# Convolution stage: the branch's early products as three fp32r products each, moved behind the fourth forward transform, and a ring of three PSUM banks

## The reference, cut to what matters

```python
y_a = _hyena(zx[..., :OFF_Q], ...)         # for o, gate in (x1, x2): y = gate * (irfft(rfft(y) * kf[o]) + bias * y)
y_b = _window_attention(q, k, v, kc, vc, attn_sink)
x_new = x + g1 * ((ga * (y_a @ w_branch_a) + gb * (y_b @ w_branch_b)) @ w_out)
x_new = x_new + g2 * _expert_choice(...)   # 16 experts, top-k of the tokens each
```

## Time and profile before

| what | us |
|---|---|
| median of 3 runs (2128.19 to 2129.42) | 2128.59 |
| the profiled execution's own time | 2128.68 |
| its span in the trace | 2126.8 |
| PE busy in the span | 2088.9 |
| convolution stage, 677.3 to 828.4: its length | 151.1 |

### The profile page before, as it was taken

The page is one execution under the profiler, slowest core; times in us unless marked ns, Lnnn a source line. Parts: engine busy times, 40 slices in busy tenths (PEclk is TensorE's granted clock), DMA queues, the critical chain, the costliest instruction groups (busy, mean ns, idle before and its releaser), DMA issues.

```text
span 2126.8 us, 28086 instructions
## 1 busy us (share of the span) xinstructions
PE 2088.9 (98%) x10361; PEld 1689.1 (79%) x10361; DVE 1667.5 (78%) x1784; ACT 1205.9 (57%) x1321; POOL 243.3 (11%) x106
## 2 busy tenths in 40 slices
PE   8999999989999999999999999999999999999998
PEld 6988888866679785787688888888888888888886
DVE  4577765158885987855898988889988989889986
ACT  4521222156622332334487787777877777877875
POOL 2000000000000012200620222102220122102200
PEclk9999999999999999999899999999999999999999
DMA  9144454130012457443899999999999999999993
GB/s 330 35 128 167 137 187 152 50 130 16 16 50 109 139 139 252 149 177 100 329 400 409 401 401 401 389 399 384 374 379 397 392 377 377 382 404 380 381 375 110
DMA packets 191371, 547.98 MB, mean 258 GB/s; under 512 B 17069, under 2 KB 67599, under 8 KB 190656
## 3 DMA queue, kind: packets, MB, share of 16 engines
q1 hardware_dynamic: 179512, 508.92, 63.5%
q0 software_dynamic: 6992, 23.29, 4.7%
q10 hardware_dynamic: 4792, 14.74, 1.9%
HBM read 504.97 MB, written 35.66 MB: 254 GB/s over the span
## 4 chain that ended last, share of the span: by engine, by line
PE 72%; DVE 3%; DMA 2%; ACT 1%; issue 1%; POOL 0%; POOLq 0%; SPq 0%; ACTq 0%; DVEq 0%
PE p_y L347 6%; PE p_y L349 5%; PE p_y L348 5%; PE p_b L347 5%; PE p_b L349 5%; PE p_b L348 5%; PE p_a L347 5%; PE p_a L349 5%; PE p_a L348 5%; PE p_j L1634 2%; PE p_m L347 2%; PE p_m L349 2%; PE p_m L348 2%; PE p_acc L2019 2%; PE p_o L1519 2%; PE p_t L3177 1%
## 5 line engine op out<-in xcount | busy, mean ns | idle before, releaser
L3044 DVE TENSOR_TENSOR r_lo<-ring,r_hi 128x2048 fp32r<-128x2048 f32 x372 | 838.8, 2287 | 57.5 <-ACT r_hi L2992 56.3
L2992 ACT ACTIVATE r_hi<-ring 128x2048 fp32r<-128x2048 f32 x372 | 708.5, 1916 | 149.3 <-PE p_b L349 72.9
L347 PE MATMUL p_y<-r_hi,a_hi 128*128 128x512 f32 x512 | 205.3, 401 | 0.0
L349 PE MATMUL p_y<-r_hi,a_lo 128*128 128x512 f32 x512 | 200.0, 391 | 0.0
L348 PE MATMUL p_y<-r_lo,a_hi 128*128 128x512 f32 x512 | 199.2, 389 | 0.0
L347 PE MATMUL p_a<-r_hi,x_hi 128*128 128x512 f32 x500 | 198.6, 397 | 0.0
L347 PE MATMUL p_b<-r_hi,x_hi 128*128 128x512 f32 x504 | 196.7, 390 | 0.1
L348 PE MATMUL p_b<-r_lo,x_hi 128*128 128x512 f32 x504 | 196.1, 389 | 0.0
L349 PE MATMUL p_b<-r_hi,x_lo 128*128 128x512 f32 x504 | 196.1, 389 | 0.0
L349 PE MATMUL p_a<-r_hi,x_lo 128*128 128x512 f32 x500 | 195.1, 390 | 0.0
L348 PE MATMUL p_a<-r_lo,x_hi 128*128 128x512 f32 x500 | 194.6, 389 | 0.0
(11 more groups left out here) (441 smaller groups left out, 3868.9 us busy)
## 6 DMA issues: line engine op xcount, KB each, us to landing
ring<-in_w_gate SPq DMA_DIRECT2D x128, 1024.0 KB, 10.7
ring<-in_w_up SPq DMA_DIRECT2D x128, 1024.0 KB, 10.0
ring<-in_w_down SPq DMA_DIRECT2D x128, 1024.0 KB, 12.6
ada_rest<-in_ada_w SPq DMA_DIRECT2D x16, 1024.0 KB, 5.4
w_raw<-in_w_in SPq DMA_DIRECT2D x15, 1024.0 KB, 7.4
h_parts<-in_ada_w SPq DMA_DIRECT2D x16, 512.0 KB, 9.1
gate_dram<-zs ACTq DMA_DIRECT2D x16, 512.0 KB, 2.6
x_normed<-gate_dram SPq DMA_DIRECT2D x16, 512.0 KB, 4.3
```

What stands on the lines that cost most here:

```text
L347: pe.matmul(out, a_hi, b_hi, start=start, stop=False)
L349: return pe.matmul(out, a_lo, b_hi, start=False, stop=stop)
L2992: act.activation(r_hi[:, i % PARTS], ring[:, i % RAW], ACT.Copy).then_inc(hi_ready, 1)
L3044: dve.tensor_tensor(r_lo[:, i % PARTS], ring[:, i % RAW], r_hi[:, i % PARTS].bitcast(F32), ALU.subtract).then_inc(lo_ready, 1)
```

## The change

`branch(j)` uses `three` on `w2_hi`/`w2_lo` and on the split `y2`: twelve fp32r matmuls of 512 columns in place of four fp32 ones, into one bank of `p_branch`. ACT makes the high parts (`rows_high` once, `columns_high(j)` eight times, into a single buffer `w2_hi`, so that it waits for the branch before), DVE the low parts (`rows_low` once, `columns_low(j)` eight times), and `branch(j)` waits for its low part. The freed bank goes to `pj`, a ring of three. The branches move: none ahead of forward 2; 0 after forward 3; two after each pair; 6 and 7 after back 6. SP's queue puts the loads of the merge's operands and of the gates in another order.

```diff
-        pj = ps("p_j", [P, 2, 512])
-        p_b = ps("p_branch", [P, 2, 512])
+        pj = ps("p_j", [P, BANKS, 512])
+        p_b = ps("p_branch", [P, 512])
...
             load_gate(0)
             load_columns(2)
+            load_gate(1)
             load_columns(3)
             load_columns(4)
-            load_gate(1)
-            load_columns(5)
             load_merge_input(0, g["yb"][:, :, 512:L], g["yb_dram"][:, 512:L])
             load_gate(2)
+            load_columns(5)
+            load_merge_input(1, g["wa"][:], A["w_branch_a"][0])
             load_columns(6)
-            load_merge_input(1, g["wa"][:], A["w_branch_a"][0])
+            load_merge_input(2, g["wb"][:], A["w_branch_b"][0])
             load_gate(3)
             load_columns(7)
-            load_merge_input(2, g["wb"][:], A["w_branch_b"][0])
...
-                        pe.wait_ge(emptied, n - 1)
+                        pe.wait_ge(emptied, n - BANKS + 1)
...
             def branch(j):
-                if j == 0:
-                    pe.wait_ge(y2_in, 16)
-                pe.wait_ge(w2_in[j % 2], 16 * (j // 2 + 1))
-                if j >= 2:
-                    pe.wait_ge(branch_read, j - 1)
+                pe.wait_ge(early_low, j + 3)
+                if j:
+                    pe.wait_ge(branch_read, j)
                 for c in range(NCH):
-                    mm = pe.matmul(p_b[:, j % 2], w2[:, j % 2, c, :], y2[:, c, :], start=c == 0, stop=c == NCH - 1)
+                    high = y2_halves[c // 2][1]
+                    mm = three(pe, p_b[:], w2_hi[:, c, :], w2_lo[:, j % 2, c, :], high[:, c % 2], y2_lo[:, c, :],
+                               c == 0, c == NCH - 1)
                 mm.then_inc(branch_done, 1)
 
             forward(0)
             forward(1)
             turn(1)
-            pe.wait_ge(spectrum_read, S_LAST - 2)
-            branch(0)
-            branch(1)
-            branch(2)
             forward(2)
             back(pe, 0)
             forward(3)
+            branch(0)
             back(pe, 1)
-            branch(3)
+            branch(1)
             turn(2)
             forward(4)
             back(pe, 2)
+            branch(2)
             forward(5)
             back(pe, 3)
-            branch(4)
+            branch(3)
             turn(3)
             forward(6)
             back(pe, 4)
+            branch(4)
             forward(7)
             back(pe, 5)
             branch(5)
+            back(pe, 6)
             branch(6)
-            back(pe, 6)
             branch(7)
...
+            def rows_high():
+                act.wait_ge(y2_in, 16)
+                act.wait_ge(spec_ready, 4)
+                for part, high in y2_halves:
+                    act.activation(high, y2[:, part], ACT.Copy).then_inc(early_high, 1)
+
+            def columns_high(j):
+                act.wait_ge(w2_in[j % 2], 16 * (j // 2 + 1))
+                if j:
+                    act.wait_ge(branch_done, j)
+                act.activation(w2_hi[:], w2[:, j % 2], ACT.Copy).then_inc(early_high, 1)
...
+            transformed(2)
+            rows_high()
+            columns_high(0)
+            transformed(3)
             branch_copy(act, 0)
+            columns_high(1)
             branch_copy(act, 1)
-            branch_copy(act, 2)
-            transformed(2)
-            transformed(3)
-            branch_copy(act, 3)
+            columns_high(2)
...
             transformed(7)
             branch_copy(act, 5)
+            columns_high(6)
+            branch_copy(act, 6)
+            columns_high(7)
...
+        def rows_low(dve):
+            for n, (part, high) in enumerate(y2_halves):
+                dve.wait_ge(early_high, n + 1)
+                dve.tensor_tensor(y2_lo[:, part], y2[:, part], high.bitcast(F32), ALU.subtract).then_inc(early_low, 1)
+
+        def columns_low(dve, j):
+            dve.wait_ge(early_high, j + 3)
+            dve.tensor_tensor(w2_lo[:, j % 2], w2[:, j % 2], w2_hi[:].bitcast(F32), ALU.subtract).then_inc(early_low, 1)
...
+                if k == 2:
+                    rows_low(dve)
+                    columns_low(dve, 0)
...
+                if k == 7:
+                    columns_low(dve, 7)
...
             for k in range(N):
                 spectral(k)
+                if 2 <= k <= 6:
+                    columns_low(dve, k - 1)
                 if k >= 2 and k % FC == 0:
                     gating(dve, k // FC - 1)
+                if k == 6:
+                    columns_low(dve, 6)
```

More of the change, by code:

```diff
@@ L1931, in convolve @@
     ident, ya, tf, ti = g["ident"], g["ya"], g["tf_again"], g["ti"]
-    SETS = 2 * ORD
+    SETS, BANKS = 2 * ORD, 3
     N = SETS * FC
@@ L1942, in convolve @@
         gate = sb("gate_in", [P, 2, L])
+        with ExitStack() as below:
+            sbb, _ = g["scope"](below)
+            y2_lo, w2_lo = sbb("yb_early_lo", [P, NCH, 512], F32R), sbb("wb_columns_lo", [P, 2, NCH, P], F32R)
         y2 = sb("yb_early", [P, NCH, 512])
         w2 = sb("wb_columns", [P, 2, NCH, P])
+        w2_hi = sb("wb_columns_hi", [P, NCH, P], F32R)
+        first_tables = g["tf_lo"][:, 0:NCH // 2].rearrange("p t c n -> p t (c n)")
+        y2_halves = (slice(0, NCH // 2), g["yb_r"][:, 0:NCH // 2, 0:512]), (slice(NCH // 2, NCH), first_tables)
         staged = g["hid"]
         first_ut = g["fpm"][:].rearrange("p a q (h n) -> p a q h n", h=FC)
-        pj = ps("p_j", [P, 2, 512])
-        p_b = ps("p_branch", [P, 2, 512])
+        pj = ps("p_j", [P, BANKS, 512])
+        p_b = ps("p_branch", [P, 512])
         acc = ps("p_acc", [P, 2, 4, LQ])
@@ L1953, in convolve @@
         filled, emptied, b_done = sem("bank_filled"), sem("bank_emptied"), sem("back_done")
+        early_high, early_low = sem("branch_early_high"), sem("branch_early_low")
         x_read = sem("x_read")
@@ L2036, in turn_half @@
                 n = first_bank("turn", i) + 2 * par + q2
-                if n >= 2:
-                    pe.wait_ge(emptied, n - 1)
+                if n == BANKS - 1:
+                    pe.wait_ge(spectrum_read, S_LAST - 2)
+                if n >= BANKS:
+                    pe.wait_ge(emptied, n - BANKS + 1)
                 for h in range(FC):
@@ L2042, in turn_half @@
                         to = HC * h + P * j
-                        mm = pe.transpose(pj[:, n % 2, to:to + P],
+                        mm = pe.transpose(pj[:, n % BANKS, to:to + P],
                                           ya[:, 2 * (i % 2) + j, at:at + 4 * P - 3:4], ident[:])
@@ L2050, in turned_half @@
                 act.wait_ge(filled, n + 1)
-                act.activation(values_at(i)[:, par, q2].rearrange("p h n -> p (h n)"), pj[:, n % 2], ACT.Copy)\
+                act.activation(values_at(i)[:, par, q2].rearrange("p h n -> p (h n)"), pj[:, n % BANKS], ACT.Copy)\
                    .then_inc(emptied, 1)
@@ L2067, in forward @@
                         n = first_bank("forward", k) + 2 * odd + bank
-                        pe.wait_ge(emptied, n - 1)
+                        pe.wait_ge(emptied, n - BANKS + 1)
                         for z in range(2):
                             q = 2 * bank + 1 if odd else 2 * (bank ^ z)
-                            mm = class_sum(pe, pj[:, n % 2, HC * z:HC * z + HC], tf[:, 2 * q + z],
+                            mm = class_sum(pe, pj[:, n % BANKS, HC * z:HC * z + HC], tf[:, 2 * q + z],
                                            values_at(i)[:, odd, q // 2], c)
@@ L2120, in branch_copy @@
                 act.wait_ge(branch_stored, 16 * j)
-            act.activation(staged[:], p_b[:, j % 2], ACT.Copy).then_inc(branch_read, 1)
+            act.activation(staged[:], p_b[:], ACT.Copy).then_inc(branch_read, 1)
             act.wait_ge(branch_read, j + 1)
@@ L2139, in transformed @@
                         into = (cp, cp_other)[bank][:, odd].rearrange("p (a z n) -> p a z n", a=2, z=2)
-                        found = pj[:, n % 2].rearrange("p (z n) -> p z n", z=2)
+                        found = pj[:, n % BANKS].rearrange("p (z n) -> p z n", z=2)
                         act.activation(into[:, 0], found, ACT.Copy)
@@ L2149, in convolve_scalar @@
             turned(1)
+            transformed(2)
+            rows_high()
+            columns_high(0)
+            transformed(3)
             branch_copy(act, 0)
+            columns_high(1)
             branch_copy(act, 1)
-            branch_copy(act, 2)
-            transformed(2)
-            transformed(3)
-            branch_copy(act, 3)
+            columns_high(2)
             turned(2)
             transformed(4)
+            branch_copy(act, 2)
+            columns_high(3)
             transformed(5)
-            branch_copy(act, 4)
+            branch_copy(act, 3)
+            columns_high(4)
             turned(3)
             transformed(6)
+            branch_copy(act, 4)
+            columns_high(5)
             transformed(7)
             branch_copy(act, 5)
+            columns_high(6)
+            branch_copy(act, 6)
```

(2 more changed lines are left out.)

## The result

The changed kernel takes 2135.13 us in the median (2133.42 to 2136.63, 8 runs) against 2128.39 (2126.78 to 2130.19, 8 runs) for the kernel before, measured beside it: ratio 1.0031, 95% interval 1.0021 to 1.0041. It is **slower by 6.7 us**; the forecast was 2135.5 us, with a range of 2130 to 2140. The profiled execution took 2135.6 us with a span of 2133.7, 6.9 more than the span before.

The account below looks back on a forecast made before the run. TensorE was taken as the bound, with VectorE's loop of nearly equal length beside it. Stage end +8.0, merge -2.8 and clock +1.7 gave +6.9 on 2128.68, stated as 2135.5 us, range 2130 to 2140.

Parts of the forecast that it names:

- Step 1: Branches on PE: three fp32r products take 2.72 us per branch instead of 3.44, 5.7 us less over eight.
- Step 2: Forward 2 without early branches: PE stands until ACT's copies, back 0 6.1 us earlier; another 3 us wait in forward 3.
- Steps 3 and 4: Low parts in k = 2: PE stands 2.5 us before branch 1, 1.5 lost by turn 2; then 1.4 more per pair.
- Step 5: End of the stage: columns_low(6) waits for high part 6, PE stands 5.3 us before branch 7, back 7 8.0 late.
- Step 6: Loads of the merge's operands: issuing the last one earlier costs and gives nothing.
- Step 7: In the merge: late parts start about 836.5, both of PE's waits for DVE vanish, 2.8 us given back.
- Step 8: PE's clock: one fall to half behind the stop at the stage's end, +1.7 us, bounds 0 and 3.4.
- A: The forecast, late low parts and late k = 7, with or without the clock: +5.2 to +8.6 us; chance 0.65.
- C: PE's sum decides: the stops don't arise and the kernel is faster, -9.7 us, 2119.0; chance 0.08.
- B: Smaller lateness: columns_low(6) and (7) come 3 us earlier, the clock stays, +2.2 us, 2130.9; chance 0.17.
- D: Slow low parts or late gates make DVE the merge's bound, nothing given back: +11.2 us, 2139.9; chance 0.10.
- E: Third bank does nothing, ACT's copies pace the turns at 3.3 us: +1.2 to +2 on A; part of A and D.

Follow-up runs that it names:

- e1: The changed kernel with four fp32 matmuls per branch again and no high or low parts: 2130.74 us, 1.0016 of the kernel before.
- e3: The changed kernel with two buffers for the columns' high parts, each made ahead of the branch copies on ACT: 2130.62 us, 1.0018 of the kernel before.
- e7: The kernel before with only SP's order of loads changed, the merge's last operand loaded earlier: 2126.07 us, 0.9986 of the kernel before.
- e11: The kernel before with only SP's order of loads changed, run again: 2126.88 us, 0.9985 of the kernel before.
- e5: The kernel before with only the ring of three banks for p_j and one bank for p_branch: 2130.47 us, ratio 1.0015.
- e2: The changed kernel with four thrown-away fp32 matmuls put in front of branch 7: 2133.5 us, 1.0029 of the kernel before.
- e4: The changed kernel with the ring of p_j at two banks again, p_branch still in one: 2139.55 us, 1.0053 of the kernel before.
- e9: The changed kernel with fp32 branches moved into PE's stops, no high or low parts, and the old order of loads: 2124.64 us, 0.9974 of the kernel before.
- e6: The changed kernel with fp32 branches moved into PE's stops, no high or low parts, new order of loads: 2124.97 us, 0.9978 of the kernel before.

## Why the prediction was right, and where its terms were off

- **Step 1 (products), mis-sized.** A branch takes 725.94 - 723.05 = 2.89 us, not 2.72: the first matmul behind an fp32 transform takes 723.41 - 723.05 = 0.36 instead of 0.23. That is 0.84 of fp32. PE had more than that in stops, so it mattered little. The Trainium skill's four passes for true fp32 ("FP8 and Floating Point Precision", TensorE Precision Notes) would make three products 0.75 of it; the measured 0.84 is further from that than the forecast's 0.79.
- **Step 2 (the stop in forward 2), right.** 5.67 us against 5.7, DVE's sum at 700.98 to 703.3 as taken. The 3 us of waiting in forward 3 did not show, because back 0 and the end of forward 2 ran at half the clock and used it up. The last eight passes of forward 2 took 708.07 - 704.50 = 3.57 us and back 0 took 8.10, together 3.0 more than at full clock. In e1, with the same stop, the lower level lasted only 3.4 us, and 1.22 of the wait was left. That the fall behind this stop is covered was the forecast.
- **Steps 3 and 4, right by 0.7 us.** The stop before branch 1 was 2.42 (2.5 forecast), turn 2 at 738.30 (738.1), turn 3 at 774.77 (774.1). The turn still waits 1.11 us for ACT at 741.00; the forecast had it 0.4 shorter, and it took 741.59 - 738.30 = 3.29.
- **Step 5 (the end), right and the largest.** High part 6 ends at 812.8 (812.0), k = 7 starts at 813.46 (812.6), the stop is 5.21 (5.3). Back 7 starts at 832.39; by the forecast 829.4 and 1.7 for the clock are 831.1. e3 shows that high part 6 carries 3.6 of the 7.6 us, and e1 that undoing the products takes off 5.1, nearly all of it in this joint.
- **Step 6 (order of loads), its reasoning failed.** "Costs and gives nothing" is wrong on the kernel before, where the order gives 3 us (e7, e11). The prediction looked at who uses the operand, PE with no wait, and not at what is queued behind ACT's wait of 11.12 us: the copies and stores of branches 6 and 7, for which the late parts waited until 834.36. Both rows stood in the earlier trace rows, and step 7 used the second without asking what made it late. In the changed kernel this did not hurt the sum, since lateness alone gives back the same microseconds: e5 has the old order of loads and a back 7 that is 5.1 us late, and its stretch from back 7 to the merge's first fp32r matmul is 32.25 us, as short as in e7. The changed kernel's ACT comes to its early parts only at 822.39, later than the late load let them start before (817.87). No run has the changed kernel with the old order.
- **Step 7 (given back), mechanism right.** 3.21 us were given back instead of 2.8. The late parts start at 839.50, not 836.5, as the gating waits for back 7; DVE is still not PE's bound.
- **Step 8 (clock), right in size, in part by luck.** It is 1.8 us by e2, where 1.7 were forecast, within the bounds. But two errors cancelled: the lower level lasted 6.8 us, twice the 3.4 taken from the earlier trace rows, and 2.9 of that lay in the stop itself, where it costs nothing. Behind the same length of stop in e4 more of it lay on work, and it cost 2.7. The clock was at 0.50 around both 705 and 826, which agrees with what the prediction drew from the Trainium skill ("TensorE: Matmul & The Clock Gate", "What's actually happening"): that the throttled level is the default and activity releases it.
- **The sum.** L: back 7 is 832.39 - 677.24 - (821.45 - 677.10) = 10.8 late (1.8 of it the clock), less 3.2 is +7.6, where the forecast had 9.7 less 2.8 = +6.9. The span grew by 6.9 and the median by 6.7, so some 0.7 went later, against the prediction's word that the shift stays. The trace shows one place: at 1021.34 the kernel before waits 1.26 us for a gather's DMA, and the changed kernel passes it at 1028.08 without a wait. That the time came out within 0.4 us of the forecast is luck: a longer back 7, more given back and this later gain cancel.
- **The rivals.** A came true. C falls by the trace, since all the stops arose, and by e1. B's condition was made true in e3 (columns_low(6) and (7) come 4.2 us earlier), but the clock did not stay: +3.2 in L, 1.6 of it the clock, and a ratio of 1.0018, where B had +2.2. D didn't arise: the merge's waits are gone. E falls by e4.

## What to carry to other kernels

Faster products on the leading engine were worth nothing here, where their preparation lands on the engines that it takes turns with; price the joint where the last prepared part is needed, through every queue that it passes. Branches without dependences belong where the leading engine stands anyway: taking them out of such a place uncovers the stop, and the fall of the clock behind it. Ask of every wait, harmless for its user or not, what is queued behind it on its engine: a load for which PE never waited held up two stores behind ACT's wait and cost 3 us.

## What the runs showed of the hardware unexpectedly

- PE's granted clock fell to the lower level around stops of 1.83 us (e3), 4.34 (e5) and 5.21 and 5.67 (changed), and not around the one of 2.42. It lasted 3.4 us in e3, in e5 and, in e1, around the same stop of 5.67 that had 6.8 us in the changed kernel. In e3 and e5 it began only after PE had started again, so the length of a stop alone did not tell what the fall cost: between branch 7 and back 7 it was 1.6 us in e3, 1.8 in the changed kernel and in e5, and 2.7 in e4 behind the same 5.21 us of stop. The rows of e5's clock, whose stop ended at 819.54:

```profile
818.00:820.00 2.00, 0.46 (x1) 0.30 (x2) 2.00 (x5) 1.40 (x3) 0.55 (x3) 0.95 0.35 78
820.00:822.00 2.00, 2.00 (x4) 0.70 (x3) 0.41 (x1) 0.00 (x0) 0.00 (x0) 0.50 0.85 254
822.00:824.00 2.00, 2.00 (x5) 0.95 (x4) 0.00 (x0) 0.00 (x0) 0.00 (x0) 0.69 0.99 302
```

  Filling the stop with idle multiplications (e2) kept it at 1.00 and gave 1.8 us.
- A third PSUM bank was worth 2.4 us on PE's path up to back 6 under the changed order, and 3.3 us of L with the clock (e4); the waits that differ are those of 6.02 and 1.35 in the forward transforms (5.67 and none with three) and of 1.59 and 0.20 in a turn (1.11 with three).
- From the issue of an accumulating DMA of 512 KB to its reader's start were 5.4 us in the kernel before, 6.3 in e9, and 7.5 in e6 with a load of 2 MB issued 2.5 us behind it; but 5.6 in e7 with the same load 1.4 us behind it. What made the difference stays open.
